# RWKV-7 pairs on one core: half of the 64 by 64 products cross between the partition halves

## The chip, the core and the metric

One core of one Trainium2 chip runs the whole program in one launch. The time is device microseconds (us), from the first to the last instruction. The kernel before took 2040.35 us, the median of three runs (2037.23 to 2043.66). The engines are TensorE (PE; its weight loads are shown apart as PEld), VectorE (DVE), ScalarE (ACT), GpSimd (POOL) and SyncE (SP, which issues the DMAs).

## The reference

The program is a trunk of two layers on 512 tokens of width 1024: a bidirectional RWKV-7 mixer, then a latent attention, each followed by a mixture of 16 experts. The change touches the RWKV mixer alone, whose recurrence runs for 16 heads of width 64 in both directions:

```python
def step(state, inp):
    r_t, w_t, k_t, v_t, a_t, b_t = inp
    sa = jnp.einsum('bhij,bhj->bhi', state, a_t)
    state = (state * w_t[:, :, None, :] + sa[..., None] * b_t[:, :, None, :]
             + v_t[..., None] * k_t[:, :, None, :])
    y_t = jnp.einsum('bhij,bhj->bhi', state, r_t)
    return state, y_t
...
for direction in range(2):
    ...
    y = y + wkv7_scan(r_h, decay, k_d, v_h, -kk, kk * a_h, reverse=(direction == 1))
```

## The kernel before

The kernel does the recurrence in chunks of 64 tokens, for one pair of heads at a time (8 pairs, u). A pair has 2 heads (h) by 8 chunks by 2 directions (d). Chunk c is called by its tile m = c // 2 (four tiles of 128 tokens) and its half p = c % 2: the tokens of half p lie in partitions 64p to 64p+63. Nearly all products of a pair are 64 by 64, so a matmul uses a quarter of TensorE's array: the row half is where its operands lie in SBUF, the column half where its result lies in PSUM. One fp32 matmul of the program is two MATMUL and two LDWEIGHTS records in the trace; a transpose is one of each.

In the order of TensorE's own program, a pair is:

1. **Scores.** `across` makes the masked products LR (line 831), L (878), LR of the other direction, and the bonus (884). Then 128 by 128 transposes (822, `turn`) bring v, a, b and k of both directions into token order, with the MR products (831) between them, and the small projections w0 and a0 of the next pair (562).
2. **Inversion.** Five levels. A level is one X job, one T job and one U job for each direction, each 16 matmuls (32 records): X = block times T, T = U times X, U = X times U. VectorE adds the unit matrix to X on its way out of PSUM (1270), ScalarE copies T (1131) and U (1134 and 1137). T and X are made by `inverse_step` (853) into two banks; from level 1 on the chunks of head 1 are left in the other partition half by X and brought back by T. U of levels 1 to 3 (957) is written into one bank and stays in its half: chunks use only the two array quarters whose row and column halves are equal. Between the jobs stand matmuls of the next pair's projections: k and r (545), w1 and a1 (562), v.
3. **At level 2** also the transposes of the previous pair's output (yT), and the masked keys times values, x0 (863, `within`), one job for each direction, in banks 6 and 7.
4. **Right sides and states.** PQ (977) is U times the turned a and x0; then N (989, 999), ZM (1008), corrections (1018, 1027).
5. **Chain and outputs.** Seven steps of the state chain (1058), n = 1 to 7, which VectorE scales in one direction (1306) and ScalarE in the other (1160). `out_part` (1040) adds four products to the outputs between the steps: one after step 1, one after step 2, two after step 3. It too uses only two quarters.

Each engine runs its own program in order; the order above is written out by hand. A PSUM bank is handed over by two counters: `open_job` waits until the bank's former user was read, `job_full` until it is written. The `Jobs` table gives each job its bank. VectorE also makes the next pair's operands at the levels: at level 2 reciprocal and rates (610 to 633), at level 3 the operands (638 to 649) and the last pair's output (1225, 1227), at level 4 the second direction's.

After the eighth pair SyncE waits for that pair's output before it begins to load the experts' weights, and output projection, experts, attention and experts follow one another.

## Time and profile before

| | us |
|---|---|
| median of the runs (lowest, highest) | 2040.35 (2037.23, 2043.66) |
| span of the profiled execution | 2041.4 |
| TensorE busy in the span | 1867.2 |
| VectorE, ScalarE, GpSimd busy | 802.7, 516.7, 239.0 |

The profiled execution lies 1.05 us above the median and inside the spread of the runs; nothing is counted around its span. A busy TensorE is one with any matmul under way, which says nothing of how many quarters of the array work. So for the pairs one reads how long a job of 32 records takes, and what ended the idle time in front of a row (`[us <-releaser]`); "issue" there is time in which the engine waited for nothing that the profile shows.

### The profile page before, as it was taken

Reading aid. Unit: us, or ns where it says so; the run is one execution under the profiler, and the core shown is the slowest. Engines: PE = TensorE matmul, PEld = TensorE weight load, DVE = VectorE, ACT = ScalarE, POOL = GpSimd, SP = SyncE. Lnnn points to the kernel's source line nnn. Section 1 sums busy time; section 2 is a strip of 40 time slices with the busy share of each in tenths; the row PEclk is TensorE's granted clock in tenths of the full one; section 3 lists DMA queues with packets and bytes.
Section 4 is the critical chain, followed back from the end, with each engine's and each line's share of the span. In section 5 each row is a group of like instructions: output and inputs, shape, how many; then the busy total and the mean of one; then the engine's idle time right before and its main releaser. Section 6 shows DMA issues by size and latency. Waiting matters only on the chain.

```text
span 2041.4 us, 43949 instructions
## 1 busy us (share of the span) xinstructions
PE 1867.2 (91%) x19544; PEld 1004.0 (49%) x19544; DVE 802.7 (39%) x1448; ACT 516.7 (25%) x1001; POOL 239.0 (12%) x294
## 2 busy tenths in 40 slices
PE   7899999999998959999988889899895999998987
PEld 4476766766767524333333336566543433333332
DVE  7855755655654241222211113676714122221211
ACT  2344344344343110110110112555511101101010
POOL 2203213213213110000000001211111000000000
PEclk9999999999999989999999999899997999999999
DMA  4101101101103459999999990300036999999997
GB/s 121 35 3 38 44 9 38 44 8 38 44 8 118 188 218 400 428 428 427 428 428 427 427 389 1 115 23 23 12 140 272 384 427 428 426 429 428 426 428 320
DMA packets 85861, 459.92 MB, mean 225 GB/s; under 512 B 16805, under 2 KB 49962, under 8 KB 61354
## 3 DMA queue, kind: packets, MB, share of 16 engines
q1 hardware_dynamic: 83658, 449.78, 54.2%
q0 software_dynamic: 2016, 7.34, 0.9%
q8 instruction: 155, 2.54, 0.5%
q14 instruction: 32, 0.26, 0.0%
HBM read 449.23 MB, written 7.86 MB: 224 GB/s over the span
## 4 chain that ended last, share of the span: by engine, by line
PE 61%; DMA 20%; DVE 6%; issue 5%; ACT 3%; DVEq 2%; SPq 1%; POOL 1%; POOLq 1%; ACTq 0%; PEldq 0%; another core or an unknown queue 0%
DMA arena<-in_moe_w_down 17%; PE banks L1639 13%; PE bank L545 8%; PE banks L1342 5%; PE banks L853 5%; PE bank L1639 4%; PE bank L1685 3%; DMA arena<-in_moe_w_up 2%; ACT arena L2174 2%; PE banks L957 2%; PE banks L1685 2%; PE banks L1040 1%; PE banks L977 1%; PE banks L831 1%; PE banks L2159 1%
## 5 line engine op out<-in xcount | busy, mean ns | idle before, releaser
L1639 PE MATMUL banks<-arena 128*64 128x512 f32 x2560 | 566.4, 595 | 27.0 <-DMA arena<-in_moe_w_up 14.7
L1639 PEld LDWEIGHTS banks<-arena 128*64 128x64 f32 x2560 | 182.8, 137 | 374.2 <-issue 342.6
L1742 DVE TENSOR_TENSOR arena<-arena,bank 128x512 f32<-128x512 f32 x80 | 55.0, 688 | 320.8 <-PE bank L1685 320.8
L545 PE MATMUL bank<-arena 128*128 128x512 f32 x336 | 166.2, 616 | 1.5 <-DVE arena L1270 0.7
L1188 POOL TENSOR_TENSOR arena<-arena 128x512 f32<-128x512 f32 x80 | 101.5, 1293 | 456.7 <-DVE arena L1245 456.7
L1639 PE MATMUL bank<-arena 128*64 128x512 f32 x512 | 119.2, 616 | 24.5 <-DMA arena<-in_moe_w_down 24.5
L853 PE MATMUL banks<-arena 64*64 64x64 f32 x5632 | 127.7, 223 | 13.8 <-issue 7.4
L853 PEld LDWEIGHTS banks<-arena 64*64 64x64 f32 x5632 | 112.1, 135 | 51.4 <-issue 38.2
L1698 ACT ACTIVATE arena<-banks 128x512 f32<-128x512 f32 x32 | 19.1, 597 | 411.0 <-PE banks L1639 411.0
L1731 DVE SCALAR_TENSOR_TENSOR arena<-arena,banks 128x512 f32<-128x512 f32 x32 | 33.7, 1052 | 206.5 <-PE banks L1639 206.5
L1342 PE MATMUL banks<-arena 128*128 128x512 f32 x256 | 112.6, 595 | 1.8 <-POOLq L401 1.3
L1270 DVE TENSOR_TENSOR arena<-banks,arena 128x512 f32<-128x512 f32 x80 | 51.7, 685 | 135.2 <-PE banks L853 134.5
L1715 POOL DMA_INDIRECT arena<-out_dram,small x14 | 13.6, 968 | 778.9 <-DVE small L1721 717.5
L1728 DVE SCALAR_TENSOR_TENSOR arena<-arena,banks 128x512 f32<-128x512 f32 x32 | 22.0, 687 | 186.8 <-ACT arena L1698 186.8
L1639 PEld LDWEIGHTS bank<-arena 128*64 128x64 f32 x512 | 39.8, 141 | 102.5 <-issue 90.8
L545 PEld LDWEIGHTS bank<-arena 128*128 128x128 f32 x336 | 57.6, 189 | 56.0 <-issue 49.5
L1685 PE MATMUL bank<-arena 128*128 128x512 f32 x160 | 77.7, 600 | 3.0 <-ACTq L1707 3.0
L1342 PEld LDWEIGHTS banks<-arena 128*128 128x128 f32 x256 | 47.6, 190 | 58.6 <-issue 58.6
L1701 ACT COPY arena<-bank 128x512 f32<-128x512 f32 x32 | 18.7, 585 | 205.8 <-PE bank L1658 205.8
L1131 ACT COPY arena<-banks 128x512 f32<-128x512 f32 x64 | 37.5, 586 | 88.4 <-PE banks L853 88.4
L957 PE MATMUL banks<-arena 64*64 64x64 f32 x1536 | 54.8, 218 | 2.9 <-issue 2.8
L957 PEld LDWEIGHTS banks<-arena 64*64 64x64 f32 x1536 | 50.2, 135 | 5.3 <-issue 5.2
(351 smaller groups left out, 2582.2 us busy)
## 6 DMA issues: line engine op xcount, KB each, us to landing
arena<-in_moe_w_gate SPq DMA_DIRECT2D x64, 2048.0 KB, 35.6
arena<-in_moe_w_up SPq DMA_DIRECT2D x64, 2048.0 KB, 37.6
arena<-in_moe_w_down SPq DMA_DIRECT2D x58, 2048.0 KB, 39.1
arena<-in_moe_w_down SPq DMA_DIRECT2D x16, 512.0 KB, 20.7
out_dram<-arena SPq DMA_DIRECT2D x12, 512.0 KB, 2.7
arena<-in_x SPq DMA_DIRECT2D x8, 512.0 KB, 5.8
arena<-in_rw_wr SPq DMA_DIRECT2D x8, 512.0 KB, 4.3
arena<-in_rw_wk SPq DMA_DIRECT2D x8, 512.0 KB, 6.3
```

The lines of the kernel that those rows point to most:

```text
L545: last = nc.tensor.matmul(b[:, :], w_sl[:, n, k, :], xmix[n][:, k, :], start=(k == 0), stop=(k == ND - 1))
L853: last = nc.tensor.matmul(v[swapped(p, h, lands), h, token(m)], st(q, h, m), mv(q, h, m), start=True, stop=True)
L957: last = nc.tensor.matmul(b[q, (h * NT + m) * CH:(h * NT + m + 1) * CH], xs(q, h, m), us(q, h, m), start=True, stop=True)
L1131: nc.scalar.copy(Tm[:, :, d, :], two_banks(("T", lv, d, u))).then_inc(free[rj[("T", lv, d, u)][0]], 1)
L1188: nc.gpsimd.tensor_tensor(blocks[lv][d].rearrange("p h m j -> p (h m) j"), LRB[d].rearrange("p h m a j -> p (h m) a j")[:, :, 0, :], bc(le ...
L1270: nc.vector.tensor_tensor(Xm[d].rearrange("p (h m) j -> p h m j", h=2), two_banks(name).rearrange("p h (m j) -> p h m j", j=CH), bc(eye.un ...
L1342: last = nc.tensor.matmul(b[:, :], yT[n][:, k, tile(t)], wo_at[n][:, k, z * 512:(z + 1) * 512], start=(k == 0), stop=(k == ND - 1))
L1639: last = nc.tensor.matmul(b[z * CAP:(z + 1) * CAP, :], st[:, k, :], ring[g % RING][:, k, z * 512:(z + 1) * 512], start=(c % 2 == 0 and k = ...
L1685: nc.tensor.matmul(b[:, :], combT[:, t * P:(t + 1) * P], ye[:, z * 512:(z + 1) * 512], start=True, stop=True).then_inc(full[COMB[j]], 1)
L1731: nc.vector.scalar_tensor_tensor(hid[e].rearrange("p (k q) -> p q k", k=4), th.rearrange("p (q k) -> p q k", k=4), 0.5, b[:, :].rearrange( ...
L1742: nc.vector.tensor_tensor(xs, xs, b[:, :], ALU.add).then_inc(free[COMB[j]], 1)
L2174: nc.scalar.activation(prob[h][:, t, :], b[:, :], ACT.Exp, bias=nmx[:, n:n + 1], scale=q_scale[u % 2][:, 2 * t + h:2 * t + h + 1], accum_o ...
```

## The change

The names change first: all eight banks are one tensor. Then:

- `inverse_step` takes for each job which chunks are read from the other half (`there`) and which are left there (`lands`). After level 0 U leaves head 1's chunks swapped, after level 1 those of odd tiles, and so on in turn. A chunk that moves goes to the second bank of a job, one that stays to the first, so that in every job from U of level 0 on half of the chunks cross. U of levels 1 to 3 takes two banks.
- x0 is one job of 32 matmuls for both directions in banks 6 and 7, and its result for head 1 lands swapped; ScalarE reads it with four copies in place of two. The transposes yT move behind U of level 2 on TensorE, and their reading by ScalarE (`y_feature`) behind the copies of level 2.
- The turned a is made by 16 matmuls of 64 by 64 against the unit matrix (`turn_by_heads`) in place of four transposes, and the turns and MR jobs are put in another order.
- PQ and `out_part` use all four quarters; the outputs of head 1 are swapped back by ScalarE in two copies of 64 partitions.

```diff
@@ -501,21 +500,22 @@
         for u in range(NPAIR):
             order += [(("LR", 0, h, u), 2 + h) for h in range(2)] + [(("L", h, u), 6 + h) for h in range(2)]
             order += [(("LR", 1, h, u), 4 + h) for h in range(2)]
-            order += [(("bonus", u), 0), (("vt", u), 1), (("at0", u), 6), (("bt0", u), 7)]
+            order += [(("bonus", u), 0), (("vt", u), 1), (("at0", u), 6)]
             order += [(("MR", 0, h, u), 2 + h) for h in range(2)]
-            order += [(("kt0", u), 0), (("at1", u), 1), (("bt1", u), 6), (("kt1", u), 7)]
+            order += [(("bt0", u), 1), (("kt0", u), 0), (("at1", u), 6)]
             order += [(("MR", 1, h, u), 4 + h) for h in range(2)]
+            order += [(("bt1", u), 6), (("kt1", u), 7)]
             more = u < NPAIR - 1
             for piece in FILL[:4] if more else []:
                 order += prep_jobs(piece, u)
-            order += [(("yT", u), 7)] if u else []
-            order += [(("x0", 0, u), 6), (("x0", 1, u), 7)]
+            order += [(("x0", u), 6)] + ([(("yT", u), 7)] if u else [])
             order += prep_jobs(FILL[4], u) if more else []
             for lv in range(LEVELS):
-                order += [(("X", lv, d, u), 2 * d) for d in range(2)]
+                here, other = (0, 4) if lv % 2 == 0 else (4, 0)
+                order += [(("X", lv, d, u), (here, 2)[d]) for d in range(2)]
                 if lv < LAST:
-                    order += [(("T", lv, d, u), 2 * d) for d in range(2)]
-                order += [(("U", lv, d, u), {0: (4, 0), LAST: (0, 4)}.get(lv, (4, 5))[d]) for d in range(2)]
+                    order += [(("T", lv, d, u), (here, 2)[d]) for d in range(2)]
+                order += [(("U", lv, d, u), (here, other)[d] if lv == LAST else (other, here)[d]) for d in range(2)]
             order += [(("PQ", d, h, u), 2 * d + h) for d in range(2) for h in range(2)]
             order += [(("N", d, u), 4 + d) for d in range(2)]
             order += [(("ZM", d, p, u), 2 * d + p) for d in range(2) for p in range(2)]
...
-
-        def swapped(p, h, there):
-            return half[1 - p if there and h else p]
+            return all_banks[:, b * 512:(b + 2) * 512].rearrange("p (h n) -> p h n", h=2)[:, :, 0:NT * CH]
+
+        KEEP, HEADS, TILES = (lambda h, m: 0), (lambda h, m: h), (lambda h, m: m % 2)
+        LEVEL_PLACE = [KEEP, HEADS, TILES, HEADS, TILES, HEADS]
+
+        def slots(there, lands):
+
+            move = lambda h, m: there(h, m) ^ lands(h, m)
+            by_bank = [[(h, m) for h in range(2) for m in range(NT) if move(h, m) == bank] for bank in range(2)]
+            if not by_bank[1]:
+                by_bank = [[(h, m) for m in range(NT)] for h in range(2)]
+            return {hm: (bank, n) for bank in range(2) for n, hm in enumerate(by_bank[bank])}
+
+        def step_slots(kind, lv):
+
+            if lv < 0:
+                return slots(KEEP, KEEP)
+            if kind == "X":
+                return slots(KEEP, LEVEL_PLACE[lv])
+            return slots(LEVEL_PLACE[lv], KEEP if kind == "T" else LEVEL_PLACE[lv + 1])
+
+        FINAL = step_slots("U", LEVELS - 1)
 
         def inverse_step(pe, name, there, lands, st, mv):
 
             open_job(pe, rj, name)
             v = two_banks(name)
+            at = {z: hm for hm, z in slots(there, lands).items()}
+            for n in range(NT):
+                for bank in range(2):
+                    h, m = at[bank, n]
+                    for p in range(2):
+                        q = half[p ^ there(h, m)]
+                        last = nc.tensor.matmul(v[half[p ^ lands(h, m)], bank, token(n)], st(q, h, m), mv(q, h, m), start=True, stop=True)
+            last.then_inc(full[rj[name][0]], 1)
+
+        def turn_by_heads(pe, d, u):
+
+            open_job(pe, rj, (f"at{d}", u))
+            v = two_banks((f"at{d}", u))
             for m in range(NT):
-                for h in range(2):
-                    for p in range(2):
-                        q = swapped(p, h, there)
-                        last = nc.tensor.matmul(v[swapped(p, h, lands), h, token(m)], st(q, h, m), mv(q, h, m), start=True, stop=True)
-            last.then_inc(full[rj[name][0]], 1)
...
-            b = open_job(pe, rj, name)
-            for h in range(2):
+                for p in range(2):
+                    for h in range(2):
+                        last = nc.tensor.matmul(v[half[p ^ h], h, token(m)], AR[u % 2][d][half[h], 0, 2 * m + p, :], ident[half[h], half[h]],
+                                                start=True, stop=True)
+            last.then_inc(full[rj[(f"at{d}", u)][0]], 1)
+
+        def keys_by_values(pe, u):
+
+            b = open_job(pe, rj, ("x0", u))
+            for d in range(2):
                 for m in range(NT):
                     for p in range(2):
-                        o = (h * NT + m) * w
-                        last = nc.tensor.matmul(b[half[p], o:o + w], st(half[p], h, m), mv(half[p], h, m), start=True, stop=True)
-            last.then_inc(full[rj[name][0]], 1)
+                        for h in range(2):
+                            o = (6 + h, d * NT + m)
+                            last = nc.tensor.matmul(ps[o[0]][half[p ^ h], token(o[1])], MRK[d][half[p], h, m, 0, :], vtok[half[p], m, half[h]],
+                                                    start=True, stop=True)
+            last.then_inc(full[rj[("x0", u)][0]], 1)
 
         def pairs_pe(pe):
...
-                part_a = lambda d: plain(AR[u % 2][d][:, 0, :, :].rearrange("p c j -> p (c j)"))
                 turn(pe, ("vt", u), plain(vT))
-                turn(pe, ("at0", u), part_a(0))
+                job_read(pe, rj, ("L", 1, u))
+                turn_by_heads(pe, 0, u)
+                across(pe, "MR", Kt[0], 0, u)
                 turn(pe, ("bt0", u), plain(Bt[0]))
-                across(pe, "MR", Kt[0], 0, u)
                 turn(pe, ("kt0", u), plain(Kt[0]))
-                turn(pe, ("at1", u), part_a(1))
+                turn_by_heads(pe, 1, u)
+                across(pe, "MR", Kt[1], 1, u)
                 turn(pe, ("bt1", u), plain(Bt[1]))
                 turn(pe, ("kt1", u), plain(Kt[1]))
-                across(pe, "MR", Kt[1], 1, u)
                 if more:
...
-                            turn(pe, ("yT", u), plain(ysq))
+                        job_read(pe, rj, ("vt", u))
                         for d in range(2):
-                            job_read(pe, rj, ("vt", u))
                             for h in range(2):
                                 job_read(pe, rj, ("MR", d, h, u))
-                            within(pe, ("x0", d, u), CH, lambda q, h, m: MRK[d][q, h, m, 0, :], lambda q, h, m: vtok[q, m, half[h]])
+                        job_read(pe, rj, ("kn", u) if more else ("kt1", u))
+                        keys_by_values(pe, u)
                     if lv == 3 and more:
                         prep_pe(pe, ("wa", 1), rj, u)
                     if lv == 4 and more:
...
                         if lv < LAST:
-                            inverse_step(pe, ("T", lv, d, u), lv > 0, False, us, xs)
+                            inverse_step(pe, ("T", lv, d, u), LEVEL_PLACE[lv], KEEP, us, xs)
                         if lv == 0 and d == 0:
                             for h in range(2):
                                 job_read(pe, rj, ("MR", 1, h, u))
-                        if lv in (0, LAST):
-                            inverse_step(pe, ("U", lv, d, u), lv > 0, lv == 0, xs, us)
-                        else:
-                            b = open_job(pe, rj, ("U", lv, d, u))
-                            for m in range(NT):
-                                for h in range(2):
-                                    for p in range(2):
-                                        q = swapped(p, h, True)
-                                        last = nc.tensor.matmul(b[q, (h * NT + m) * CH:(h * NT + m + 1) * CH], xs(q, h, m), us(q, h, m),
-                                                                start=True, stop=True)
-                            last.then_inc(full[rj[("U", lv, d, u)][0]], 1)
+                        inverse_step(pe, ("U", lv, d, u), LEVEL_PLACE[lv], LEVEL_PLACE[lv + 1], xs, us)
                     if lv == 0 and more:
                         for k in range(2, ND):
...
+                    job_read(pe, rj, ("x0", u))
                     job_read(pe, rj, (f"at{d}", u))
                     bs = [open_job(pe, rj, ("PQ", d, h, u)) for h in range(2)]
+                    for m in range(NT):
+                        for p in range(2):
+                            last = [nc.tensor.matmul(bs[h][half[p], m * P:(m + 1) * P], Um[d][half[p ^ h], FINAL[h, m][0], FINAL[h, m][1], :],
+                                                     AQ[d][half[p ^ h], h, m, :, :].rearrange("p a b -> p (a b)"), start=True, stop=True)
+                                    for h in range(2)]
                     for h in range(2):
-                        for m in range(NT):
-                            for q in half:
-                                last = nc.tensor.matmul(bs[h][q, m * P:(m + 1) * P], Um[d][q, h, m, :],
-                                                        AQ[d][q, h, m, :, :].rearrange("p a b -> p (a b)"), start=True, stop=True)
-                        last.then_inc(full[rj[("PQ", d, h, u)][0]], 1)
+                        last[h].then_inc(full[rj[("PQ", d, h, u)][0]], 1)
...
+                        for p in range(2):
+                            for h in range(2):
+                                last = nc.tensor.matmul(ys[h][half[p ^ h], token(m)], st(half[p], h, m), mv(half[p], h, m), start=(first and m == 0),
                                                         stop=False, skip_group_check=True)
                     return last
 
                 def out_state(n):
                     for h in range(2):
                         for d, c in ((0, n), (1, NCH - 1 - n)):
-                            last = nc.tensor.matmul(ys[h][half[c % 2], token(c // 2)], ZM[d][half[h], c % 2, c // 2, 0, :],
...
+
                 feature_major = lambda v, n: v[:, :, :, n, :].rearrange("p h m j -> p m h j")
                 turned("vt", flat(vtok))
-                turned("at0", feature_major(AQ[0], 0))
+                turned_heads(0)
                 turned("bt0", feature_major(LRB[0], 2))
                 turned("kt0", flat(ktok[0]))
-                turned("at1", feature_major(AQ[1], 0))
+                turned_heads(1)
                 turned("bt1", feature_major(LRB[1], 2))
                 turned("kt1", flat(ktok[1]))
                 if u:
...
+                        job_full(act, rj, ("x0", u))
                         for d in range(2):
-                            b = job_full(act, rj, ("x0", d, u))
-                            nc.scalar.copy(AQ[d].rearrange("p h m a j -> p (h m) a j")[:, :, 1, :], chunks(b[:, :])).then_inc(free[rj[("x0", d, u)][0]], 1)
+                            for h in range(2):
+                                last = nc.scalar.copy(AQ[d][:, h, :, 1, :], ps[6 + h][:, d * NT * CH:(d + 1) * NT * CH].rearrange("p (m j) -> p m j", j=CH))
+                        last.then_inc(free[rj[("x0", u)][0]], 1)
                     for d in range(2):
...
-                    nc.scalar.copy(ytok[:, :, h, :], b[:, 0:256].rearrange("p (t v) -> p t v", t=NT)).then_inc(free[rj[("y", h, u)][0]], 1)
+                    y = b[:, 0:256].rearrange("p (t v) -> p t v", t=NT)
+                    if h:
+                        for q in range(2):
+                            last = nc.scalar.copy(ytok[half[1 - q], :, h, :], y[half[q], :, :])
+                    else:
+                        last = nc.scalar.copy(ytok[:, :, h, :], y)
+                    last.then_inc(free[rj[("y", h, u)][0]], 1)
 
```

Two places of TensorE's program. The first is the turns of a pair, from the bonus on. L917 and L884 are the bonus, L822 the transposes, L831 MR, L562 w0 and a0. Before, then now:

```order
L884 MATMUL banks<-arena 128x512
L822 MATMUL banks<-ident,arena 128x128 x4
L822 MATMUL bank<-ident,arena 128x128 x8
L831 MATMUL banks<-arena 64x128 x16
L822 MATMUL banks<-ident,arena 128x128 x8
L822 MATMUL bank<-ident,arena 128x128 x8
L831 MATMUL banks<-arena 64x128 x16
L562 MATMUL bank<-arena 128x512 x2
```

```order
L917 MATMUL banks<-arena 128x512
L822 MATMUL banks<-ident,arena 128x128 x4
L883 MATMUL banks<-ident,arena 64x64 x16
L831 MATMUL banks<-arena 64x128 x16
L822 MATMUL banks<-ident,arena 128x128 x8
L883 MATMUL banks<-ident,arena 64x64 x16
L831 MATMUL banks<-arena 64x128 x16
L822 MATMUL banks<-ident,arena 128x128 x8
L562 MATMUL banks<-arena 128x512 x2
```

The last two turns, of b and k of direction 1, stood ahead of the second MR job and stand now between it and w0, a0, which write the banks that these turns fill. Two groups of 8 transposes became two groups of 4 and two of 16 small matmuls.

The second place is levels 2 to 4 of the first pair, from the last r matmuls (L545) to PQ (L977, now L1003). L853 and L957 (now L873) are the inversion, L863 (now L895) is x0. Before, then now:

```order
L545 MATMUL bank<-arena 128x512 x4
L853 MATMUL banks<-arena 64x64 x32
L863 MATMUL bank<-arena 64x64 x32
L853 MATMUL banks<-arena 64x64 x16
L957 MATMUL banks<-arena 64x64 x16
L853 MATMUL banks<-arena 64x64 x16
L957 MATMUL banks<-arena 64x64 x16
L853 MATMUL banks<-arena 64x64 x32
L562 MATMUL bank<-arena 128x512 x2
```

```order
L545 MATMUL banks<-arena 128x512 x4
L873 MATMUL banks<-arena 64x64 x32
L895 MATMUL banks<-arena 64x64 x32
L873 MATMUL banks<-arena 64x64 x96
L562 MATMUL banks<-arena 128x512 x2
L873 MATMUL banks<-arena 64x64 x96
L545 MATMUL banks<-arena 128x512
```

The number of matmuls is the same; T, U and the next X are now alike. In later pairs the transposes yT stood between the first X jobs and x0, and stand now after the fourth of these T and U jobs.

## Rows read from the trace of the kernel before

**Rows 1.** The page: span, engines, queues, and one group of section 5.

```profile
span 2041.4 us, 43949 instructions
...
PE 1867.2 (91%) x19544; PEld 1004.0 (49%) x19544; DVE 802.7 (39%) x1448; ACT 516.7 (25%) x1001; POOL 239.0 (12%) x294
...
q8 instruction: 155, 2.54, 0.5%
...
L853 PE MATMUL banks<-arena 64*64 64x64 f32 x5632 | 127.7, 223 | 13.8 <-issue 7.4
```

**Rows 2.** Windows of the fifth pair; columns as in the first line.

```profile
core 0: us, PE busy (x) PEld busy (x) DVE busy (x) ACT busy (x) POOL busy (x), PEclk, DMA share, GB/s
417.70:424.30 6.60, 6.60 (x137) 4.31 (x136) 0.00 (x0) 4.16 (x6) 0.00 (x0) 1.00 0.01 2
424.30:441.50 17.20, 15.49 (x587) 13.04 (x586) 15.29 (x22) 9.73 (x17) 0.00 (x0) 1.00 0.06 19
441.50:452.90 11.40, 10.96 (x274) 8.30 (x266) 7.72 (x17) 3.99 (x8) 0.00 (x0) 1.00 0.01 3
```

**Rows 3.** Timeline of TensorE, fifth pair, levels 2 to 4: start us, us, what.

```profile
424.36 1.16 PE L853 MATMUL banks<-arena 64*64 64x64 f32 x64
...
426.04 1.15 PE L863 MATMUL bank<-arena 64*64 64x64 f32 x32
...
430.69 1.09 PE L957 MATMUL banks<-arena 64*64 64x64 f32 x31 [0.30 <-issue]
...
434.79 0.28 PE L853 MATMUL banks<-arena 64*64 64x64 f32 x3 [0.36 <-issue]
...
438.69 0.82 PE L853 MATMUL banks<-arena 64*64 64x64 f32 x38 [0.86 <-issue]
...
440.49 1.16 PE L853 MATMUL banks<-arena 64*64 64x64 f32 x64
```

**Rows 4.** Timeline of VectorE, the same stretch.

```profile
425.12 1.29 DVE L1270 TENSOR_TENSOR arena<-banks,arena 128x512 f32<-128x512 f32 x2 [9.27 <-PE banks L853]
...
432.94 1.29 DVE L1270 TENSOR_TENSOR arena<-banks,arena 128x512 f32<-128x512 f32 x2
...
439.08 1.29 DVE L1270 TENSOR_TENSOR arena<-banks,arena 128x512 f32<-128x512 f32 x2 [0.45 <-PE banks L853]
```

**Rows 5.** Timeline of TensorE, inversion of the last pair.

```profile
642.40 0.86 PE L957 MATMUL banks<-arena 64*64 64x64 f32 x23 [1.34 <-issue]
...
646.29 1.09 PE L863 MATMUL bank<-arena 64*64 64x64 f32 x30 [0.25 <-issue]
...
650.03 1.09 PE L957 MATMUL banks<-arena 64*64 64x64 f32 x30 [0.73 <-issue]
```

**Rows 6.** Timeline of TensorE, products and state chain of the fifth pair.

```profile
442.64 3.62 PE L977 MATMUL banks<-arena 64*64 64x128 f32 x61
...
452.92 0.45 PE L1058 MATMUL banks<-arena 64*64 64x64 f32 x8 [0.47 <-DVE arena L1306]
...
453.18 1.13 PE L1040 MATMUL banks<-arena 64*64 64x64 f32 x32
...
454.11 0.43 PE L1058 MATMUL banks<-arena 64*64 64x64 f32 x8
```

**Rows 7.** Timeline of VectorE, beside the chain.

```profile
453.49 0.68 DVE L638 TENSOR_TENSOR arena<-arena 128x512 f32<-128x512 f32 x1
...
454.69 0.28 DVE L1306 TENSOR_SCALAR arena<-banks,small 128x64 f32<-128x64 f32 x1
```

**Rows 8.** Timeline of TensorE, end of the turns, fifth pair.

```profile
397.86 1.10 PE L831 MATMUL banks<-arena 64*64 64x128 f32 x32
...
398.90 1.13 PE L562 MATMUL bank<-arena 64*128 64x512 f32 x4
...
399.95 2.08 PE L853 MATMUL banks<-arena 64*64 64x64 f32 x64
```

**Rows 9.** Timeline of ScalarE, the last two copies of turned tiles.

```profile
397.62 1.09 ACT L1106 COPY arena<-bank 128x512 f32<-128x512 f32 x2
```

48 lines of the change are left out of this document (23 added, 25 removed).

## Prediction

> **What bounds the kernel now.** I read the page first, for the span and for how full TensorE is: 1867 of 2041 us [rows 1]. That says only that some matmul is always under way. Then the windows of one middle pair, the fifth: TensorE covers nearly all of each stretch at granted clock 1.00, while VectorE is idle at level 1 (0.00 of 6.60 us) and almost full at levels 2 to 4 (15.29 of 17.20) [rows 2]. The timeline then shows how long jobs take. 64 records of L853, whose second half crosses to the other partition half, take 1.16 us, and so do 32 records of x0 (1.15), which do not cross [rows 3]. A record lasts 0.22 us by itself (223 ns) [rows 1], so the rate is (1.16 - 0.22) / 64 = 14.7 ns on four quarters of the array and (1.15 - 0.22) / 32 = 29 ns on two. The change brings more jobs to the first rate, and what they save is open only where nothing else sets the end. Two other things do.
>
> The first is VectorE. From the X additions of level 2 (425.12) to those of level 4 (439.08) it is idle for 0.45 us alone [rows 4].
>
> The second is the supply of instructions. The profile has 2 x 19544 matmul and load records and 155 transfers on the instruction queue, 2.54 MB [rows 1]: one transfer of 16 KB for about 252 of them. In jobs without any wait TensorE stops for "issue": at 430.69, 434.79 and 438.69 in the fifth pair [rows 3], and at 642.40, 646.29 and 650.03 in the last [rows 5]. The distances are 4.10, 3.90, 3.89 and 3.74 us, and by the program's order 256 of TensorE's instructions stand between each two. So a block of 256 instructions needs some 3.9 us to come, one after the other. With one load and one matmul record each, a block lasts 128 x 29 ns = 3.7 us on two quarters, which the supply just feeds, and 1.9 us on four, which it can't feed for long.
>
> After the last pair SyncE begins the experts' loads only when that pair's output is written, so what the pairs gain or lose passes to the end.
>
> **The change, part by part.** Each is for one pair of the seven that also prepare a next one.
>
> *U of level 1* (two jobs of 32 records): 32 x (29 - 14.7) = 0.46 us each, 0.9 together. TensorE alone fills this stretch [rows 2], so all of it counts: **-0.9**.
>
> *Levels 2 to 4*: four U jobs (4 x 0.46 = 1.8) and x0 (128 instructions at 14.7 ns a record, 0.94 in place of 1.86; the wait of x0's second job for bank 7 goes too) free about 3.0 us of TensorE. But VectorE can move up only by its 0.45 us of idling: X of level 4 would be added from 438.63, the first of the two additions done at 439.3, and U of level 4 could start at 439.4 in place of 440.49 [rows 3, 4]: at most 1.1 us. ScalarE, with four x0 copies in place of two, is ready before that; the w1 matmul, which needs the bank of yT, waits for ScalarE's late `y_feature`, but still ends by the time VectorE allows T of level 3. Supply then takes its share: about 1190 instructions stand from X of level 2 to the end of U of level 4, 4.6 blocks. The first two are partly in store; four spacings of 3.9 us and the rest of a block give 16.0 to 16.7 us, against 17.1 now (424.36 to 441.5). I take **-0.7**, between nothing and 1.1.
>
> *PQ*: 64 records of 128 columns take 3.4 us (3.62 less the last one's length) [rows 6] and half of that on four quarters. From there to the chain 540 instructions, two blocks, have 10 us, so supply does not bind, and the VectorE and ScalarE readers of PQ are done before ZM wants them, behind 2.4 us of other matmuls: **-1.7**.
>
> *Outputs beside the chain*: each part of 32 records takes 1.13 - 0.22 = 0.91 us [rows 6], now 0.47. After step 1 this fits: the step stands 1.19 us after the first [rows 6], and could at 0.8. But then VectorE makes two operands (453.49 to 454.77) ahead of its next scaling (454.69 to 454.97) [rows 7], so step 3 gains 0.2 us only, not 0.9. The two parts after step 3 give their full 0.9. Together 1.1; supply, with 300 instructions in 3.4 us, may take part of it: **-0.8**, between 0.2 and 1.1.
>
> *The turns*: 16 small matmuls at 14.7 ns a record cost 0.47 us, the four transposes 0.44, nothing to speak of. The order costs. Before, the last copies of turned tiles ran on ScalarE from 397.62 to 398.71 [rows 9], under the second MR job, and w0, a0 started at 398.90, X at 399.95 [rows 8]. Now b and k of direction 1 are turned after MR. Two turns (0.9 us with the change of tile shape) end at 399.0, their copies at about 399.5 and 400.0, and w0, a0 may start 0.2 us after each: 399.7 and 400.2. Both together take 1.05 us, so X starts at 401.25: **+1.3**. Behind it queue X, k and T of level 0, which no other engine holds up, so all of it counts; the bound below is 0.9 (if the copies keep closer), the one above 2.4 (if w0 and a0, now apart, no longer run at once).
>
> *The rest*: two half copies for the output of head 1 and four for x0 are on ScalarE, under VectorE's work: nothing.
>
> Sum for such a pair: -0.9 - 0.7 - 1.7 - 0.8 + 1.3 = -2.8 us; seven pairs -19.6. The last pair has no w0, a0 and no projections between; supply paces it from level 1 to PQ [rows 5], so it saves mostly PQ: -2.0. In all **-21.6**. The profiled span is 2041.4 us [rows 1], so 2019.8; it lies 1.05 above the median, which gives 2018.8: **2019 us**.
>
> The Trainium skill (Runtime: NRT & Kernel Launch, section Instruction fetch mechanics) says that instructions come in 16 KiB blocks of 256, that the sequencer fetches the next while it runs the current one, and that the crossing is mostly hidden, because issue is slower than the fill. The trace agrees on the size and not on the hiding: the stops of up to 1.34 us above are such crossings. By the page's rule the supply would take nothing, which is a rival below.
>
> **The rivals.**
>
> *Supply is hidden after all.* The stops would have another cause that does not grow. Then levels 2 to 4 give 1.1 and the outputs 1.1: -3.5 us a pair, 7 x 3.5 + 2.5 = -27, **2013**. For it: between 424.36 and 430.69 the dense jobs run without a stop [rows 3]. Against it: the even 3.9 us distances.
>
> *TensorE is all that counts.* Then U, x0, PQ and the outputs pay in full, 0.9 + 3.0 + 1.7 + 1.8 - 1.3 = 6.1 us a pair, 8 x 6.1 = 49: **1991**. For it: TensorE's share of every window. Against it: VectorE's packed row [rows 4].
>
> *Supply takes most.* Dense jobs follow each other more closely now, so stops come in more places, PQ and chain among them: -0.9 (level 1), nothing at levels 2 to 4, -1.2 for PQ, -0.3, +1.3, or -1.1 a pair: -8 to -9, **2031**.
>
> *Slower: supply sets every dense stretch.* Two-quarter jobs (3.7 us a block) are already at the supply's pace (3.7 to 4.1), so if that pace holds in all of the small products, four quarters bring nothing, while each pair has 112 instructions more (2 x (64 - 8), the turned a), 0.44 of a block or 1.7 us, and the 1.3 us at w0: +3.0 us, 8 pairs +24, **2064**. The point that decides: whether TensorE enters a dense stretch with instructions in store. Against it: dense jobs do run for 6 us before the first stop, and the projections between, 0.43 us a record, let the store fill.
>
> *The change does not do what it says.* Jobs that cross half of their chunks by tile would stay at 29 ns, as two chunks of one step could want one quarter or one bank. Then only the +1.3 is left, **2049**. Against it: each step of the new code names four different quarters and keeps the two row halves in two banks, as L853 does.
>
> **How the numbers follow.** Forecast 0.56, with its own range 2008 to 2028 (levels 0 to 1.1, outputs 0.2 to 1.1, turns 0.9 to 2.4, over eight pairs). Supply hidden 0.12 (2013), TensorE alone 0.07 (1991), supply takes most 0.14 (2031), supply sets everything 0.07 (2064), does nothing 0.04 (2049). The range of 2003 to 2034 leaves out the 1991, 2064 and 2049 cases, 0.18. A change of 0.3%, 6 us, is about what can be told from none: faster is below 2034.2, slower above 2046.5. Faster: 0.56 + 0.12 + 0.07 and two thirds of the 0.14, 0.84. Same: the rest of that and a little of the last two, 0.07. Slower 0.09.
>
> **What would show it.** 64 records of T and U of levels 1 to 3 in 1.16 us, and 32 of the output parts in about 0.7; level 1 shorter by 0.9 us; T of level 3 right behind VectorE's additions, which stay packed from level 2 to level 4; more idle time put down to issue than the 7.4 us of L853 now [rows 1], at distances of 3.7 to 4.1 us; PQ in half its time; w0 waiting for ScalarE's copy, and X of level 0 1.3 us later in its pair. The forecast is wrong in its parts if the stops for issue are gone, if w0 starts without a wait, or if VectorE has gaps before level 3.

## The result: 2031.05 us, faster by 0.5%, less than half of the forecast gain

| | before | after |
|---|---|---|
| median of five runs (lowest, highest), us | 2040.35 (2037.23, 2043.66) | 2031.05 (2029.76, 2034.25) |
| ratio, with its 95% interval | 1 | 0.9949 (0.9933 to 0.9965) |
| span of the profiled execution, us | 2041.4 | 2027.7 |
| in it, ahead of the first LR job | 84.3 | 82.9 |
| the 8 pairs, first LR job to step 4 of the last pair's chain | 592.2 | 576.9 |
| the rest of the span, behind them | 1364.9 | 1367.9 |

The direction and the range (2003 to 2034) hold, the size does not: 9.3 us were gained, 21 were forecast. A second set of five runs of the changed kernel gave 2030.96 against 2039.8 (0.9957, 0.9944 to 0.9970).

The profiled spans differ by more than the medians, 13.7 us. In each of the ten runs of the changed kernel the time was 2.1 us above the span (2029.76 for 2027.7), so the profiled execution of before stood at about 2043.5, 3.2 us above its median, and that of after 1.3 below its own. So of the 13.7 us, 4.5 are the spread of single executions.

One more thing differs between the two profiled executions. In the pairs TensorE ran at 1.2 GHz (granted clock 0.50) for 9.2 us before, 5.8 of them in the first pair and 3.4 in the last, and for 3.4 us after, all in the first pair:

```profile
632.80:636.20 3.40, 3.40 (x101) 3.37 (x96) 0.04 (x1) 1.75 (x3) 3.13 (x4) 0.50 0.72 276
```

That is the row of before, in its last pair (window, then the busy time of PE, PEld, DVE, ACT and POOL, granted clock, DMA share, GB/s). At half the clock these 5.8 us more are worth up to 2.9 of the 15.3 us that the pairs became shorter. In the repeated profile of the changed kernel it is the other way round: 12.4 us at 1.2 GHz. No such stretch lies in pairs 2 to 7 of the first two profiles, on which most means below rest.

### The profile page after: what moved, and what is told of

Its sections match the earlier page's. It is cut to its first block and busy times, and to the rows that moved or that the text cites. A ratio compares the mean times of both kernels' runs of the same rounds, so it can differ in the third digit from the quotient of the medians.

```text
span 2027.7 us, 44869 instructions
## 1 busy us (share of the span) xinstructions
PE 1821.4 (90%) x19992; PEld 950.3 (47%) x19992; DVE 798.6 (39%) x1448; ACT 519.5 (26%) x1025; POOL 240.1 (12%) x294
## 5 line engine op out<-in xcount | busy, mean ns | idle before, releaser
L1676 PE MATMUL banks<-arena 128*64 128x512 f32 x3072 | 685.0, 599 | 51.9 <-DMA arena<-in_moe_w_down 34.5
L1676 PEld LDWEIGHTS banks<-arena 128*64 128x64 f32 x3072 | 222.4, 138 | 478.1 <-issue 435.3
L1779 DVE TENSOR_TENSOR arena<-arena,banks 128x512 f32<-128x512 f32 x128 | 88.0, 687 | 329.8 <-PE banks L1722 329.8
L545 PE MATMUL banks<-arena 128*128 128x512 f32 x384 | 187.1, 613 | 1.3 <-ACT arena L585 1.3
L873 PE MATMUL banks<-arena 64*64 64x64 f32 x7168 | 144.1, 221 | 35.5 <-issue 28.8
L873 PEld LDWEIGHTS banks<-arena 64*64 64x64 f32 x7168 | 131.5, 134 | 78.5 <-issue 60.8
L1722 PE MATMUL banks<-arena 128*128 128x512 f32 x256 | 113.7, 597 | 3.0 <-ACTq L1744 3.0
L1768 DVE SCALAR_TENSOR_TENSOR arena<-arena,banks 128x512 f32<-128x512 f32 x32 | 33.6, 1050 | 206.8 <-PE banks L1676 206.8
L1379 PE MATMUL banks<-arena 128*128 128x512 f32 x256 | 112.6, 595 | 1.8 <-POOLq L400 1.3
L545 PEld LDWEIGHTS banks<-arena 128*128 128x128 f32 x384 | 66.5, 189 | 66.9 <-issue 58.4
L1743 ACT COPY arena<-banks 64x512 f32<-64x512 f32 x64 | 37.1, 580 | 178.6 <-PE banks L1676 178.2
L1722 PEld LDWEIGHTS banks<-arena 128*128 128x128 f32 x256 | 47.3, 190 | 59.4 <-issue 58.2
L1379 PEld LDWEIGHTS banks<-arena 128*128 128x128 f32 x256 | 47.6, 190 | 58.6 <-issue 58.6
L2047 PE MATMUL banks<-arena 128*128 128x192 f32 (+1 forms) x320 | 61.7, 347 | 1.1 <-DVE arena L1955 1.1
L2172 PE MATMUL banks<-arena 96*128 96x512 f32 x128 | 60.1, 615 | 1.6 <-POOLq L400 1.6
```

The costliest lines, as they stand in the source:

```text
L545: last = nc.tensor.matmul(b[:, :], w_sl[:, n, k, :], xmix[n][:, k, :], start=(k == 0), stop=(k == ND - 1))
L873: last = nc.tensor.matmul(v[half[p ^ lands(h, m)], bank, token(n)], st(q, h, m), mv(q, h, m), start=True, stop=True)
L1379: last = nc.tensor.matmul(b[:, :], yT[n][:, k, tile(t)], wo_at[n][:, k, z * 512:(z + 1) * 512], start=(k == 0), stop=(k == ND - 1))
L1676: last = nc.tensor.matmul(b[z * CAP:(z + 1) * CAP, :], st[:, k, :], ring[g % RING][:, k, z * 512:(z + 1) * 512], start=(c % 2 == 0 and k = ...
L1722: nc.tensor.matmul(b[:, :], combT[:, t * P:(t + 1) * P], ye[:, z * 512:(z + 1) * 512], start=True, stop=True).then_inc(full[COMB[j]], 1)
L1779: nc.vector.tensor_tensor(xs, xs, b[:, :], ALU.add).then_inc(free[COMB[j]], 1)
```

## The profile after, beside the rows of before

The page of the changed kernel:

```profile
span 2027.7 us, 44869 instructions
...
PE 1821.4 (90%) x19992; PEld 950.3 (47%) x19992; DVE 798.6 (39%) x1448; ACT 519.5 (26%) x1025; POOL 240.1 (12%) x294
...
q8 instruction: 159, 2.61, 0.5%
```

Groups by line, all of TensorE. L873 is `inverse_step` and now has U of levels 1 to 3 too, L831 is LR and MR, L822 the turns:

```profile
L873 PE MATMUL banks<-arena 64*64 64x64 f32 x7168 | 144.1, 221 | 35.5 <-issue 28.8 <-DVE arena L1307 5.8 <-ACT arena L1163 0.8
...
L831 PE MATMUL banks<-arena 64*64 64x128 f32 x1024 | 36.3, 275 | 6.8 <-issue 3.7 <-POOLq L400 3.1
...
L822 PE MATMUL banks<-ident,arena 128*128 128x128 f32 x192 | 28.1, 280 | 2.1 <-issue 1.6 <-DVE arena L1257 0.4
```

TensorE is busy for 45.8 us less than before (1867.2), close to the 49 us that the rival "TensorE is all that counts" reckoned. The idle time for issue of the same jobs was 10.2 us before, 7.4 in `inverse_step` [rows 1] and 2.8 in the U jobs, which had a line of their own; it is 28.8 now:

```profile
L957 PE MATMUL banks<-arena 64*64 64x64 f32 x1536 | 54.8, 218 | 2.9 <-issue 2.8
```

It has also appeared in LR, MR and the turns (3.7 and 1.6 us), whose MATMUL rows had none. So most of what the array no longer needs is spent waiting for instructions.

Windows of the fifth pair (level 1; levels 2 to 4; PQ to the third output part); they answer to [rows 2]:

```profile
core 0: us, PE busy (x) PEld busy (x) DVE busy (x) ACT busy (x) POOL busy (x), PEclk, DMA share, GB/s
410.40:416.05 5.65, 5.65 (x137) 3.40 (x136) 0.00 (x0) 3.96 (x6) 0.00 (x0) 1.00 0.01 3
416.10:434.30 18.20, 14.12 (x589) 10.94 (x588) 16.71 (x24) 10.58 (x20) 0.00 (x0) 1.00 0.05 18
434.35:445.90 11.55, 10.54 (x374) 8.54 (x374) 8.34 (x20) 4.01 (x9) 0.00 (x0) 1.00 0.02 4
```

TensorE's timeline there (start us, us, what, idle time before):

```profile
416.12 1.16 PE L873 MATMUL banks<-arena 64*64 64x64 f32 x64
417.17 1.16 PE L895 MATMUL banks<-arena 64*64 64x64 f32 x64
...
420.55 1.03 PE L873 MATMUL banks<-arena 64*64 64x64 f32 x51 [1.06 <-issue]
...
425.54 2.48 PE L873 MATMUL banks<-arena 64*64 64x64 f32 x130 [1.22 <-DVE arena L1307]
429.47 1.16 PE L873 MATMUL banks<-arena 64*64 64x64 f32 x62 [1.45 <-issue]
...
433.11 0.27 PE L873 MATMUL banks<-arena 64*64 64x64 f32 x2 [0.34 <-issue]
...
434.37 1.98 PE L1003 MATMUL banks<-arena 64*64 64x128 f32 x64
436.17 0.64 PE L1017 MATMUL banks<-arena 64*64 64x64 f32 x32
```

All 64 records of x0 (L895) take 1.16 us, which 32 took before [rows 3], and PQ (L1003) takes 1.98 us where it took 3.62 [rows 6]: the four quarters work. X of level 2 and x0, 256 instructions, go through in 2.0 us (416.12 to 418.12) without a stop. T of level 3 (425.54) waits for VectorE, which has no gap from the additions of level 2 on, as in [rows 4]:

```profile
424.70 1.29 DVE L1307 TENSOR_TENSOR arena<-banks,arena 128x512 f32<-128x512 f32 x2
...
430.31 1.28 DVE L1307 TENSOR_TENSOR arena<-banks,arena 128x512 f32<-128x512 f32 x2
```

This is so in three of pairs 2 to 7 (waits of 1.2 to 1.6 us). In the other three TensorE does not wait there: it had stood for issue for 2.0 to 2.5 us since X of level 2, and was late itself.

The last pair has no projections between its jobs. Where [rows 5] showed stops of 0.25 to 1.34 us, every block has one now, and they are longer:

```profile
621.46 1.50 PE L873 MATMUL banks<-arena 64*64 64x64 f32 x86 [1.79 <-issue]
...
625.01 2.21 PE L873 MATMUL banks<-arena 64*64 64x64 f32 x127 [0.81 <-issue]
628.70 0.62 PE L873 MATMUL banks<-arena 64*64 64x64 f32 x25 [1.48 <-issue]
...
632.63 1.61 PE L873 MATMUL banks<-arena 64*64 64x64 f32 x91 [1.77 <-issue]
```

By the program's order 256 instructions stand between each two, and the distances are 3.55, 3.69 and 3.93 us.

At the end of the turns of the fifth pair, where [rows 8] had MR, w0 with a0, and X without a gap:

```profile
390.44 0.49 PE L822 MATMUL banks<-ident,arena 128*128 128x128 f32 x3 [0.32 <-issue]
390.86 1.87 PE L562 MATMUL banks<-arena 64*128 64x512 f32 x4
392.66 1.56 PE L873 MATMUL banks<-arena 64*64 64x64 f32 x46
```

The four records of w0 and a0 take 1.87 us in place of 1.13: the copies of the turned tiles [rows 9] end one behind the other, and the two products no longer run at once.

I read both traces against the program's order of TensorE's instructions. In each, the first instruction of every 256 (position 193 of TensorE's stream, counted modulo 256) begins late more often than any other. The time from the end of the records in front to that instruction, summed over the 8 pairs, is what I call stops below: **11.2 us before, 39.0 after** (38.0 in the second profile). Worked out from the starts of the matmul records, means over pairs 2 to 7 in us; x-y is from the start of x to the start of y:

| step | before | forecast | after | again | e1 | e5 | e6 | e7 | e10 |
|---|---|---|---|---|---|---|---|---|---|
| first LR - X of level 0 | 10.26 | +1.3 | 12.17 | 12.22 | 11.36 | 12.67 | 12.17 | 11.40 | 11.40 |
| T of level 1 - X of level 2 | 6.58 | -0.9 | 5.66 | 5.66 | 5.66 | 5.66 | 5.66 | 5.66 | 5.66 |
| X of level 2 - PQ | 18.41 | -0.7 | 17.61 | 17.77 | 17.73 | 17.80 | 17.10 | 16.75 | 17.84 |
| PQ - keys | 3.35 | -1.7 | 1.79 | 1.79 | 1.89 | 2.21 | 1.74 | 1.70 | 1.84 |
| keys - chain | 6.85 | 0 | 6.90 | 6.82 | 7.00 | 6.85 | 6.91 | 6.89 | 7.60 |
| chain with outputs | 4.61 | -0.8 | 3.72 | 3.56 | 3.56 | 3.93 | 3.73 | 3.72 | 3.73 |
| whole pair | 76.16 | -2.8 | 73.93 | 73.91 | 73.29 | 75.21 | 73.39 | 72.21 | 74.14 |
| stops in the first of these steps | 0.00 | | 0.63 | 0.55 | 0.43 | 1.08 | 0.63 | 0.50 | 0.08 |
| all 8 pairs | 592.2 | -21.6 | 576.9 | 578.3 | 572.6 | 586.8 | 572.1 | 564.3 | 580.5 |

"Again" is the repeated profile of the changed kernel. The keys are the first matmuls behind PQ, and "chain with outputs" ends where the gate product begins, behind the last two output parts. The rest of the pair stays at 17.8 us (X of level 0 to T of level 1) and 8.3 us (end of the chain) in all. Of the profiles in this table "again", e1, e6 and e10 have one stretch of 3.4 us at 1.2 GHz in pairs 2 to 7 each, worth up to 0.3 us in a mean; that of "again" lies in the first step of the sixth pair.

## The experiments

All start from the changed kernel unless said otherwise. A ratio is to the kernel before, in the same set of runs; the changed kernel's is 0.9949 and 0.9957.

**e1: the turns of direction 1 ahead of its MR products**, as they stood in the kernel before, so that their copies run under MR (the table of banks and the waits of the jobs behind follow).

```diff
-                across(pe, "MR", Kt[1], 1, u)
                 turn(pe, ("bt1", u), plain(Bt[1]))
                 turn(pe, ("kt1", u), plain(Kt[1]))
+                across(pe, "MR", Kt[1], 1, u)
```

> The changed kernel with the turns of b and k of direction 1 put ahead of the second MR job again, in banks 1 and 0, so that their copies run under MR and w0, a0 need not wait for them. In the profile of the changed kernel X of level 0 starts 11.4 to 13.0 us after the start of a pair, against 10.2 before. Theory (the order of the turns costs this): X at 10.3 to 10.6 again, 1.3 us a pair or more, the whole 8 to 12 us faster than the changed kernel, about 2021. Rival (the supply of instructions sets the start of a pair too): TensorE then only reaches the next block earlier and stops there; X at 11 or later, less than 4 us in all, 2027 to 2031.

Measured: 2025.2 us, 0.9916 (0.9904 to 0.9929). The wait of w0, a0 for ScalarE is gone, and they run at once again:

```profile
385.46 1.31 PE L831 MATMUL banks<-arena 64*64 64x128 f32 x32
386.70 1.13 PE L562 MATMUL banks<-arena 64*128 64x512 f32 x4
387.76 2.08 PE L873 MATMUL banks<-arena 64*64 64x64 f32 x64
```

So this order costs time, and the wait was its cause. But X of level 0 stands at 11.36, not at the 10.3 of before: 0.8 of the 1.9 us came back, and 1.1 have another cause, of which the stops (0.43 left here) are a part. By the ratios e1 gives 7 to 8 us, a little under what I expected.

**e2 and e3: one X job of each direction done twice**, at level 3 and at level 1, in the seven pairs with preparation: 64 matmul records more, 0.93 us of TensorE at 14.7 ns.

```diff
-            for n in range(NT):
+            for n in [n for n in range(NT) for _ in range(times)]:
...
+                                     ..., times=2 if lv == 3 and more else 1)
```

> The changed kernel with every matmul of the two X jobs of level 3 done twice (same result; 128 more of TensorE's instructions a pair, 0.94 us of its time), in seven pairs. There TensorE waits about 1 us for VectorE at T of level 3. Theory (supply: some 3.8 us for 256 instructions in the dense stretch): half a block more, 1.0 to 1.9 us a pair, 7 to 13 us slower than the changed kernel, about 2041, with the loss at X and U of level 4 and not at T of level 3. Rival (only the engines count): hidden behind VectorE, 0 to 2 us in all, 2031 to 2033.

> The same doubling in the X jobs of level 1, where long matmuls of the projections stand around and TensorE has no slack. Both theories: its own 0.94 us in each of seven pairs, 6.6 us slower, 2037 to 2038; by supply not much more, since the blocks there last 6 to 7 us. If the doubling at level 3 costs clearly more than this one, only supply explains it.

Measured: e2 2041.97 us, 0.9993 (0.9980 to 1.0006), e3 2040.94, 0.9987 (0.9976 to 0.9998). At level 1, X to T takes 0.93 us more (X of level 0 to T of level 1, 18.73 for 17.80): there TensorE alone sets the end. At level 3, X of level 2 to T of level 3 goes from 9.52 to 10.13, so 0.3 of the 0.93 us were free. The waits of T of level 3 for VectorE, 0.7 us a pair in the mean, are gone in all six pairs, and the stops in front of it went from 1.39 to 1.68 us: VectorE and the supply share this stretch. Behind it, from T of level 3 to PQ, nothing was lost (8.19 us for 8.09 and 8.27), where my theory had put the loss; and e2 does not cost clearly more than e3. So neither "supply alone" nor "hidden" holds. Against the first profile of the changed kernel both cost 4.6 to 5.7 us in the pairs; by the ratios it is 6 to 9 us.

**e4: U of levels 1 to 3 issued bank by bank**, so that two quarters at a time should work, as before the change.

```diff
+            by_bank = name[0] == "U" and 0 < name[1] < LAST
-            for n in range(NT):
-                for bank in range(2):
+            for n, bank in ([(n, b) for b in range(2) for n in range(NT)] if by_bank else ...):
```

> The changed kernel with the U jobs of levels 1 to 3 issued bank by bank: first all chunks that stay, then all that cross, so that only two quarters of the array work at a time, with the same instructions. Each U job then takes 0.93 us, not 0.47: 2.8 us of TensorE's time a pair. Theory (VectorE and supply cover levels 2 to 4): level 1 loses its 0.9 us, levels 2 and 3 at most 0.5, 8 to 11 us slower in all, 2039 to 2042. Rival (TensorE's time counts in full): 22 us slower, 2053. Rival (supply covers all of it): under 3 us.

Measured: 2036.36 us, 0.9968 (0.9957 to 0.9980). That is 2 to 4 us slower than the changed kernel, well under my theory (8 to 11) and near the rival that supply covers all of it (under 3). Level 1 gave back 0.42 of its 0.92 us; e5 suggests why only half. Levels 2 to 4 gave back nothing, and their stops fell from 2.5 to 1.5 us a pair (in the whole 31.7 us for 39.0): there the slower jobs only fill a wait for instructions.

**e5: PQ and the output parts issued head by head**, the same matmuls in another order.

```diff
-                    for m in range(NT):
-                        for p in range(2):
-                            last = [nc.tensor.matmul(...) for h in range(2)]
+                    for h in range(2):
+                        for m in range(NT):
+                            for p in range(2):
+                                last[h] = nc.tensor.matmul(...)
```

> The same matmuls as in the changed kernel, but PQ and the six output parts of each pair are issued head by head, so that two quarters of the array work at a time instead of four; the two row halves of one step still cross. By my terms: PQ's step 1.6 us longer, the chain to its end 0.8 to 0.9 longer, 2.5 us a pair, 8 pairs +20 us, near 2052 where the changed kernel has 2032. TensorE alone: 1.74 for PQ and 6 parts of 0.45 us, +4.4 a pair, +35 us, 2067. Supply takes most: the time given back only lengthens jobs that stood at stops for issue, so the stops in PQ, keys and chain shrink (they are 1 to 2 us a pair in the first and last), and the price is +8 to +12 us, 2042.

Measured: 2039.43 us, 0.9991 (0.9981 to 1.0002), pairs 586.8 us: some 8 us, where my terms said 20. (For TensorE alone I had counted six output parts, but a pair has four: 1.74 + 4 x 0.45 = 3.5 us a pair, 28 and not 35.) The 8 us are what my third case gave, by luck. It is not the supply that covers it, as my third case had it: the steps themselves hardly grew, PQ by 0.42 us and the outputs by 0.2 to 0.4, and the stops are 37.6 us in all, hardly fewer. The start of a pair, which the edit does not touch, has 0.5 us more, all of it stops. TensorE's timeline shows why; L1005 is PQ and L1018 the keys product that stands behind all of PQ in the program:

```profile
439.03 2.26 PE L1005 MATMUL banks<-arena 64*64 64x128 f32 x58
441.03 0.27 PE L1018 MATMUL banks<-arena 64*64 64x64 f32 x1
441.13 0.28 PE L1005 MATMUL banks<-arena 64*64 64x128 f32 x2
441.14 0.22 PE L1018 MATMUL banks<-arena 64*64 64x64 f32 x1
```

A later matmul starts before an earlier one of another quarter. As I read it, a quarter that is free takes its next work while the others still have a queue; the rows show the starts, and PQ's 0.42 us, not the reason. So "head by head" does not keep two quarters idle, and e4 and e5 are only part of an undo. The Trainium skill (TensorE: Matmul & The Clock Gate, Part 3, "The mechanism") says that matmuls are strictly first in, first out in start and end, with no reordering; for starts of 64 by 64 tiles these rows show otherwise.

**e6: the normalization of the next pair's keys (L610 to L633 on VectorE, its root on ScalarE) at level 1** instead of level 2.

```diff
                     if lv == 1 and more:
                         prep_dve(dve, ("kn",), rj, u, (u + 1) % 2)
-                    if lv == 2 and more:
                         prep_dve(dve, ("kkn",), rj, u, (u + 1) % 2)
                         prep_dve(dve, ("rate", 0), rj, u, (u + 1) % 2)
```

> VectorE's small operations of the next pair's key normalization (norm and reciprocal) run at level 1 of the inversion, where VectorE is idle, instead of at level 2; nothing else moves. VectorE sets the end of levels 2 to 4: they get shorter by what is taken out, 0.3 to 0.9 us a pair (from X of level 2 to T of level 3, 9.52 us in the changed kernel), 7 pairs, -2 to -6 us. Supply sets it: the stretch keeps its 9.5 us, or the shortening comes back at U of level 4 and at PQ as stops for issue; 0 to -1 us. Slower side: X additions of level 2 come behind the moved operations, +0.2 a pair.

Measured: 2023.16 us, 0.9915 (0.9902 to 0.9928), by the ratios 7 to 9 us faster than the changed kernel, more than the 2 to 6 expected; the pairs show 4.8. VectorE's timeline, fifth pair; the reciprocal of 3.35 us now ends before the additions of level 2:

```profile
406.39 3.35 DVE L610 RECIPROCAL arena<-arena 128x512 f32<-128x512 f32 x1 [0.70 <-ACT arena L575]
...
414.05 1.29 DVE L1308 TENSOR_TENSOR arena<-banks,arena 128x512 f32<-128x512 f32 x2 [1.10 <-PE banks L873]
```

X of level 2 to T of level 3 falls from 9.52 to 8.61 us and `inverse_step`'s wait for VectorE from 5.8 to 1.1 us over the program:

```profile
L873 PE MATMUL banks<-arena 64*64 64x64 f32 x7168 | 146.2, 223 | 30.3 <-issue 28.5 <-DVE arena L1308 1.1 <-ACT arena L1165 0.8
```

So VectorE did set that stretch, as the prediction had it. Of the 0.91 us, 0.2 to 0.4 come back between T of level 3 and PQ (8.49 for 8.09 and 8.27). The stops stay at 36.7 us.

**e7: e1 and e6 together.**

> The turns ahead of the second MR part (7 us below the changed kernel before) and the moved normalization together. If both gains are of different stretches they add: the changed kernel's time minus 7 minus what the moved normalization gives alone, 2019 to 2025 us. If the supply of instructions is what is left as the bound, the second adds nothing to the first: 2025 to 2027. Start of the pair (first small product to X of level 0) as with the turns alone, 11.4 us.

Measured: 2020.71 us, 0.9891 (0.9877 to 0.9904), the fastest of all. The pairs take 564.3 us, 12.6 less than after. The two gains in the pairs (4.3 and 4.8) add to 9.1. That e7 has more than this need not be their doing, since TensorE ran at 1.2 GHz for 13.7 us of the pairs in e1's profile and 10.2 in e6's, but for 3.4 in e7's and in that of after.

**The changed kernel again**, beside e5 to e7.

> The changed kernel once more, as the control of the three kernels beside it. Its ratio was 0.9949 [0.9933, 0.9965]. If that ratio belongs to the kernels, it comes again within 0.9930 to 0.9968. If the part of the gain that is lost outside the pairs (3 us after the last pair in the profiled run) is the luck of one profiled run, this profile has the pairs at 576 to 578 us again and the rest within 1.5 us of the kernel before (1364.9); if the change causes it, the rest is again near 1367.9.

Measured: 2030.96 us, 0.9957 (0.9944 to 0.9970); pairs 578.3, rest 1366.5. The rest is 1.6 us longer than before here and 3.0 in the first profile, so neither of my two cases holds as put.

**e8: one whole block of instructions more in the last pair**: its X jobs of levels 1 and 3 done twice (edit as in e2, `times=2 if lv in (1, 3) and not more`).

> The last pair alone, on top of the changed kernel: the X jobs of levels 1 and 3 issue each matmul twice (same result), 128 matmul records and 128 loads more, one whole block of 256 instructions. From X of level 1 to PQ the changed kernel needs 23.5 us there. TensorE's rate sets it: 128 x 14.7 ns, +1.9 us. VectorE sets it: less, 0 to +1. The supply of instructions sets it: one more spacing between boundaries, +3.6 to +4.1 us. The pairs before it do not change.

Measured: X of level 1 to PQ takes 27.41 us; after had 23.51, which gives +3.9. But five other kernels with the changed one's inversion in the last pair took 22.87 to 25.16 there (e9, e5, e7, e6, the repeat; mean 24.4), so the price is +3.0, from +2.3 to +4.5. The array's 1.9 us lies below all of this, but the price alone does not decide: in this profile TensorE ran at 1.2 GHz for 3.4 us of the stretch, worth up to 1.7 us. The row, columns as above:

```profile
637.40:640.90 3.50, 3.50 (x122) 3.24 (x124) 0.69 (x1) 1.09 (x2) 0.00 (x0) 0.51 0.02 5
```

What decides is the spacing. Stops in e8:

```profile
621.18 2.09 PE L873 MATMUL banks<-arena 64*64 64x64 f32 x127 [2.06 <-issue]
624.86 2.28 PE L873 MATMUL banks<-arena 64*64 64x64 f32 x127 [1.59 <-issue]
628.84 1.51 PE L873 MATMUL banks<-arena 64*64 64x64 f32 x88 [1.70 <-issue]
```

3.68 and 3.98 us apart. From the boundary at 621.18 to that at 647.75 there are seven spacings, 3.80 us in the mean; in the changed kernel (621.46 to 644.13) six, 3.78 in the mean. The spacing that holds the slow clock is 3.92. So the addition is one spacing more and the block's pace stays, whatever is in it. No load runs beside it: the DMA queues move only instruction blocks from 626 to 642 us in the changed kernel (7 and 4 GB/s). The whole kernel: 2033.5 us, 0.9951 (0.9933 to 0.9968), which can't show 3 us.

**e9: every instruction behind the first pair's level 1 half a block further on**, by doubled X jobs of that level in that pair only (`times=2 if lv == 1 and u == 0`).

> The changed kernel with the X jobs of level 1 doubled in the first pair alone: 128 instructions more there, so that every later instruction of TensorE stands half a block further on in its stream. If the stops without a wait are block boundaries, they stay at the same place modulo 256 of the stream, that is at other instructions of the program, and the stretch from the first LR job to X of level 0, whose stops were 0.22, 1.10, 1.25, 0.32, 0.90 and 0.00 us in pairs 2 to 7, shows another pattern with a mean of again 0.3 to 0.9; without its stops it stays at 11.4 to 11.7 us. If the stops belong to instructions of the program (a wait that the profile doesn't show), pairs 2 to 7 repeat pattern and places.

Measured: the stops are still at position 193, and so at other instructions. Start of the third pair in the changed kernel, its repeat, and e9:

```profile
238.03 0.55 PE L822 MATMUL banks<-ident,arena 128*128 128x128 f32 x3
239.68 0.77 PE L822 MATMUL banks<-ident,arena 128*128 128x128 f32 x5 [1.10 <-issue]
```

```profile
237.93 0.55 PE L822 MATMUL banks<-ident,arena 128*128 128x128 f32 x3
238.68 0.77 PE L822 MATMUL banks<-ident,arena 128*128 128x128 f32 x5 [0.21 <-issue]
```

```profile
239.04 1.04 PE L831 MATMUL banks<-arena 64*64 64x128 f32 x26
240.78 0.44 PE L831 MATMUL banks<-arena 64*64 64x128 f32 x6 [0.70 <-issue]
```

The same program stops at the same instruction for another time; the shifted one stops 128 instructions further on (5 and 5, 32 and 32, 26 and 26 records, and two waits). The pattern in pairs 2 to 7 became 0.54, 0.70, 1.29, 0.04, 1.73 and 0.67 us, mean 0.83. Stops belong to blocks, not to places in the program. The whole kernel: 2035.01 us, 0.9973 (0.9962 to 0.9985), 3 to 5 us slower than the changed kernel, of which the 64 records more in the first pair explain 0.9.

**e10: less data on the DMA rings while a pair starts.** A block of instructions is a 16 KB transfer too. In the changed kernel it begins 1.2 us (median of 104) behind the boundary before it; where that boundary falls into the load of the next weights, 1.64, 3.01, 3.17, 2.80, 0.26, 2.37, 3.24 and 2.93 us. Such a delay is no proof by itself: behind some two dozen other boundaries it is over 1.6 us too, up to 8.9. So two of the three large slices were loaded when PQ is done, in the pair before.

```diff
+                if u < NPAIR - 2:
+                    job_full(sp, rj, ("PQ", 0, 0, u))
+                    weight_loads(sp, u + 2, (0, 1))
                 sp.wait_ge(full[rj[("g", u)][0]], rj[("g", u)][1])
...
-                    pair_loads(sp, u + 2)
+                    pair_loads(sp, u + 2, (2,))
```

> The changed kernel, but of the 1.7 MB of weights that arrive within 6 us from the first LR job of a pair, 1.0 MB (the r and k slices) are loaded in the pair before, when PQ of direction 0 is done; TensorE's instructions are the same. In the trace of the changed kernel a block of instructions is asked for 1.2 us (median) behind the boundary before it, but 1.6 to 3.2 us behind it in 7 of 8 cases where the boundary falls into this load. If the load delays the blocks, the stops between the first LR job and X of level 0 (0.63 us a pair in pairs 2 to 7, in the repeated run 0.55) fall to 0 to 0.3 and that stretch from 12.2 to 11.6 to 11.9; new stops may come behind PQ, 0 to 0.3 a pair. In all 0 to -4 us, near 2029. If the stops come from the density of the instructions alone, the stretch keeps 0.5 to 0.8 of stops, and the time is the changed kernel's within 0.2%.

Measured in the step: stops 0.63 to 0.08 us; the delays in pairs 2 to 7 that were 3.01, 3.17, 2.80, 2.37, 3.24 and 2.93 us are 1.90, 2.03, 2.09, 0.29, 2.10 and 2.07; first LR to X of level 0 12.17 to 11.40, in four of six pairs 11.22 or 11.23. DMA from the first LR job to X of level 0, third pair, after and then e10:

```profile
q1 hardware_dynamic: 3424, 1.70, 51.1%
q8 instruction: 2, 0.03, 1.3%
```

```profile
q1 hardware_dynamic: 1344, 0.66, 19.8%
q8 instruction: 2, 0.03, 1.1%
```

The load does delay the blocks. It only moved, though: keys to chain, where the two slices now arrive, has 0.61 us of stops for 0.03, and is 0.7 us longer. The time is 2038.71 us, 0.9987 (0.9976 to 0.9999), slower than the changed kernel and than I expected; of these 7 us the pairs show 2 to 4, the rest I can't place.

**e11: e1, e6 and e10 together.**

> The turns ahead of the second MR part, the normalization at level 1 and the early r and k weights together: the time of the first two together (ratio 0.9891, 2019 us of the profiled span) less what the early weights give alone, 0 to -4 us: 2015 to 2021 us, ratio 0.987 to 0.990. Without effect of the loads: 0.989 again. Start to X of level 0, 11.4 us with the two, 10.8 to 11.1 if the load was the cause of its 0.5 us of stops.

Measured: 2027.01 us, 0.9925 (0.9911 to 0.9938), 7 us slower than e7 (pairs 567.3 us for 564.3). First LR to X of level 0 is 10.59 us in four of six pairs (mean 10.81), 0.3 above before's 10.26: the order of the turns and the load make nearly all of the start's price. The early load doesn't pay here either.

## Why the prediction was right in its parts and wrong in its sum

The step that failed is the supply's share. The prediction took it off at levels 2 to 4 and put it at nothing, or at a mere cap, in three other places: the start of a pair, the first pair and the last pair. The runs showed 28 us more of stops at block boundaries in the pairs, and these three places cost 3.5, 1.9 and 1.0 us of the forecast gain. Term by term:

- *U of level 1*, -0.9: measured -0.92. *PQ*, -1.7: -1.56. *Outputs*, -0.8: -0.89. *Levels 2 to 4*, -0.7: -0.80, with VectorE at the end of the stretch in three of six pairs (e6 shows that it binds) and the supply in the other three.
- *The turns*, +1.3: here the supply was left out first. The term was worked out from the copies alone. e10 shows that part by itself, 11.22 for 10.26: +0.95, near the lower bound of 0.9. On top come 0.6 us of stops in pairs 2 to 7 and what they push back, +1.9 in all. The prediction let the supply take its share at levels 2 to 4 and said of the store that the projections fill it; it did not look at the start of a pair, where 1.7 MB of weights use the same DMA engines. Before, the same delays of a block (up to 3.2 us) were hidden, since TensorE needed 6.1 us for a block there; it now asks for the next after 4.6 (238.3 behind 233.7 in the third pair, the stop of 1.10 us). Six pairs by 0.6: 3.5 us of the missing gain.
- *First pair*, -2.8: measured -0.9, and up to 1.2 of that can be the clock (5.8 us at 1.2 GHz before, 3.4 after). Its stops went from 0.1 to 5.8 us (0.1 to 3.6 in the repeat); no run tested why this pair has so many. 1.9 us.
- *Last pair*, -2.0: measured -1.0 (+0.6 in the repeat). Its stops went from 3.8 to 13.3 us. I had taken supply as a pace that only caps the gain; e8 and the stops show that in this pair it sets nearly all, and the start got longer as well (8.97 to 11.33). 1.0 us. Before the change this pair held 3.4 us at 1.2 GHz, worth up to 1.7, and with the change none, so at one clock the change may have made it longer.
- Together the pairs brought -15.3 in place of -21.6, in the repeat -13.9. Counted at one clock the two lie closer: at least 12.4 and at most 15.5.
- *The account of the 12.3 us that are missing* (21.6 forecast, 9.3 measured): 6.3 in the pairs, 1.6 in the rest of the program less what the stretch ahead of the pairs gave, and the 4.5 by which the two profiled executions lie off their medians. No profile says where those last belong.
- *The rest of the program* was put at nothing and cost 1.6 to 3.0 us in the two profiles; ahead of the pairs these were 1.4 and 1.1 us shorter than before. A part can be TensorE's clock in the attention stage. After and then before, columns as above:

```profile
1319.00:1321.00 2.00, 1.82 (x8) 1.45 (x8) 1.38 (x3) 0.68 (x1) 0.89 (x3) 0.55 0.00 0
1321.00:1325.00 4.00, 4.00 (x17) 1.24 (x16) 0.75 (x1) 0.00 (x0) 0.00 (x0) 0.80 0.00 0
```

```profile
1387.00:1391.00 4.00, 4.00 (x12) 1.12 (x10) 0.65 (x1) 0.04 (x1) 0.00 (x0) 0.57 0.00 0
```

  Both kernels have such stretches of 3.4 us at 1.2 GHz, but not at the same places nor equally many: the one of after stands behind a wait of 2.1 us of TensorE. Behind the pairs the clock was at 1.2 GHz for 81.9 us after and 75.1 before; the 6.8 us more are worth up to 3.4. But the repeat has 75.5 and is still 1.6 us longer than before, so the clock is not all of it. Why one profile has more of them stays open.
- *The span*: that nothing lies around it was wrong, 2.1 us do. It did not move the forecast, which is the median less 21.6.
- *The range of the forecast itself*, 2008 to 2028, was narrower than its terms: with the three of them at their bad ends a pair gives -0.9 - 0 - 1.7 - 0.2 + 2.4 = -0.4 us, which is 2037.

Of the rivals, "supply takes most" gave 2031, the measured time, but by luck: levels 2 to 4, PQ and the outputs kept their gains, and the loss is in the starts, the first and the last pair. "Supply sets every dense stretch" named the right mechanism and only too much of it. "Hidden after all" fell with the stops, which grew by 28 us, and "TensorE alone" was right on what the array gives up (46 us) and on nothing else. The Trainium skill's rule (Runtime: NRT & Kernel Launch, "Instruction fetch mechanics") that crossing a block is mostly hidden does not hold for these jobs: 39 us of the changed kernel's pairs stand at such crossings.

What stays open: one profile each of e2, e3 and e10 shows 2 to 5 us less loss than their ratios do, e9's loss is not accounted for, and executions of one kernel spread over 4 to 14 us.

## What to carry to other kernels

When small matmuls are packed onto more of the array, count instructions and not only array time: here a stop never followed another stop in under 3.4 us in the two profiles of the changed kernel, and 256 instructions that go through faster buy stops as soon as the block in store is used up (one block went through in 2.0 us without). Look for this in every stretch that gets denser, not only where stops are already seen, and above all where large loads run, since they delay the blocks. And take the operations of another engine that can run elsewhere out of the stretch that it bounds: that (e6) and the order of the turns (e1) together gave about as much again as the change itself (e7, 2020.71 us).

## What the runs showed that I had not expected

- Blocks of instructions queue with data: with 1.7 MB of weights under way a block's transfer began 2.4 to 3.2 us behind the boundary in pairs 2 to 7, with 0.7 MB 0.3 to 2.1 us.
- Matmuls of different quarters start out of the program's order (441.03 before 441.13 above), so the order within a job matters half as much as reckoned, or less: 0.42 us in place of 0.9 for U, 0.42 in place of 1.6 for PQ.
- Half a block of shift moved each stop but left most of their sum (33.6 us over the pairs in e9, 38.0 and 39.0 in the changed kernel).
